# A decoder layer on one core: input laid out by features on the host, row factor spread by a product, first weight sums on VectorE, S5 three gaps later

## What is computed

```python
def rms_norm(x, g):
    xf = x.astype(F32)
    y = xf * lax.rsqrt(jnp.mean(xf * xf, axis=-1, keepdims=True) + EPS)
    return (y * g.astype(F32)).astype(x.dtype)
...
        xn = rms_norm(h, mix_norm_g[l])
        proj = jnp.einsum('bsd,de->bse', xn, w_in[l])
```

## Time and profile before

| | us |
|---|---|
| Median of the runs | 1942.64 |
| The profiled execution | 1942.32 |
| Its span, first to last instruction | 1939.6 |
| TensorE busy in the span | 1798.8 (93%) |
| VectorE busy | 781.7 (40%) |
| ScalarE busy | 241.8 (12%) |
| GpSimd busy | 178.6 (9%) |
| Mean granted TensorE clock | 0.971 of 2.4 GHz |

### The profile page before, as it was taken

The page is one execution under the profiler, slowest core; times in us unless marked ns, Lnnn a source line. Parts: engine busy times, 40 slices in busy tenths (PEclk is TensorE's granted clock), DMA queues, the critical chain, the costliest instruction groups (busy, mean ns, idle before and its releaser), DMA issues.

```text
span 1939.6 us, 30889 instructions
## 1 busy us (share of the span) xinstructions
PE 1798.8 (93%) x13021; PEld 1146.3 (59%) x13021; DVE 781.7 (40%) x1492; ACT 241.8 (12%) x552; POOL 178.6 (9%) x206
## 2 busy tenths in 40 slices
PE   6999999999999989999797679999999999999984
PEld 4888899889998879999642223323333333333321
DVE  7666684367457654333421112322222122221411
ACT  3012111200224421000110000000000000000021
POOL 1443342000000000000010000000000000000001
PEclk9999999999999999999898789999999999999988
DMA  6343333322121241422699999999999999999997
GB/s 221 98 140 88 99 89 89 100 66 66 47 90 55 71 171 66 162 79 66 259 377 427 426 425 425 426 426 424 421 425 424 422 425 427 425 426 421 416 411 317
DMA packets 67657, 506.13 MB, mean 261 GB/s; under 512 B 18903, under 2 KB 19051, under 8 KB 39927
## 3 DMA queue, kind: packets, MB, share of 16 engines
q1 hardware_dynamic: 49394, 476.21, 60.8%
q0 software_dynamic: 5728, 19.56, 2.9%
q10 hardware_dynamic: 12400, 8.36, 1.7%
HBM read 497.28 MB, written 14.04 MB: 264 GB/s over the span
## 4 chain that ended last, share of the span: by engine, by line
PE 71%; DMA 20%; DVE 4%; issue 2%; ACT 1%; SPq 1%; POOLq 0%; DVEq 0%; POOL 0%; ACTq 0%
PE psum L1008 20%; PE psum L1341 16%; PE psum L1011 16%; DMA arena<-in_moe_w_gate 14%; PE psum L1300 6%; PE psum L1378 4%; DMA arena<-in_moe_w_up 3%; DMA arena<-in_moe_w_down 2%; PE psum L1166 2%; DVE arena L1782 2%; PE psum L1067 1%; PE psum L1280 1%; DMA arena<-hs_rows,arena 1%; SPq L754 1%; PE psum L1197 1%
## 5 line engine op out<-in xcount | busy, mean ns | idle before, releaser
L1341 PE MATMUL psum<-arena 128*32 128x512 f32 x3584 | 416.5, 619 | 54.6 <-DMA arena<-in_moe_w_gate 26.2
L1008 PE MATMUL psum<-arena 128*128 128x128 f32 x3584 | 410.5, 276 | 0.0
L1008 PEld LDWEIGHTS psum<-arena 128*128 128x128 f32 x3584 | 405.2, 193 | 7.0 <-issue 6.4
L1782 DVE TENSOR_TENSOR arena<-psum,arena 128x512 f32<-128x512 f32 x305 | 203.3, 683 | 391.1 <-PE psum L1300 356.7
L1011 PE MATMUL psum<-arena 128*128 128x256 f32 x1456 | 322.4, 380 | 1.1 <-DVE arena L1782 1.1
L1341 PEld LDWEIGHTS psum<-arena 128*32 128x32 f32 x3584 | 119.0, 114 | 343.7 <-issue 335.4
L1011 PEld LDWEIGHTS psum<-arena 128*128 128x128 f32 x1456 | 273.6, 190 | 38.9 <-issue 2.1
L1782 DVE TENSOR_TENSOR arena<-arena,psum 128x256 f32<-128x256 f32 (+2 forms) x172 | 75.1, 437 | 415.5 <-PE psum L1008 215.6
L1378 PE MATMUL psum<-arena 128*32 128x512 f32 x1664 | 185.9, 605 | 18.8 <-DMA arena<-in_moe_w_down 18.7
L1782 DVE TENSOR_TENSOR arena<-arena 128x128 f32<-128x128 f32 (+17 forms) x452 | 181.0, 442 | 33.2 <-ACT arena L1517 25.3
L1300 PE MATMUL psum<-arena 128*128 128x512 f32 x416 | 191.9, 605 | 1.4 <-DVE arena L2425 1.4
(11 more groups left out here) (233 smaller groups left out, 1046.5 us busy)
## 6 DMA issues: line engine op xcount, KB each, us to landing
arena<-in_moe_w_gate SPq DMA_DIRECT2D x64, 2048.0 KB, 26.6
arena<-in_moe_w_up SPq DMA_DIRECT2D x64, 2048.0 KB, 24.6
arena<-in_moe_w_down SPq DMA_DIRECT2D x56, 2048.0 KB, 27.0
arena<-in_w_in SPq DMA_DIRECT2D x86, 512.0 KB, 4.6
arena<-in_w_out SPq DMA_DIRECT2D x32, 512.0 KB, 4.8
arena<-in_x SPq DMA_DIRECT2D x8, 1024.0 KB, 8.1
arena<-in_moe_w_down SPq DMA_DIRECT2D x8, 1024.0 KB, 18.5
arena<-in_moe_w_down SPq DMA_DIRECT2D x16, 512.0 KB, 12.1
```

What stands on the lines that cost most here:

```text
L1008: last = mm(B(bank, [(1, P)], off=t * P), F(a + t * P, P), F(w + i * P, P), start=start and t == 0, stop=(i == KH - 1), skip_group_check=True)
L1341: last = mm(B(bank, [(1, FE)], 32 * g, 32), F(xt + c * CAP + 32 * g, 32), F(SLOT[slot] + (c % 8) * FE, FE), start=(c == 0), stop=(c == KD ...
L1782: return v.tensor_tensor(o, a, b, op)
```

## The change

x is laid out by features on the host (`x_columns`, partition p holds features 16p to 16p+15, 512 tokens each) and loaded in six groups of 2, 2, 4, 4, 2 and 2 blocks, among the first two weight blocks. No transposes are left. VectorE multiplies each block by its gain alone (`gain`, 16 tensor_scalars of 128x512). The row factor comes later: ScalarE squares each group, GpSimd and VectorE fold the squares to 512 columns, TensorE sums them over the partitions by 28 products of one column (`square_sums`: 8 behind step k = 7, 20 ahead of k = 10), ScalarE takes the square root, VectorE the reciprocal times the identity (DIAG), and one product with ones spreads the factor over all partitions (`row_scales`, ahead of k = 12). u0 runs on the unscaled x and is scaled behind. VectorE scales A11, S1, A21, A12 and A22 by the spread factor and forms S2, S3, S4 from them. All four weight sums of the first pair are made on VectorE between these passes; disc_b and the two halves of the former lb part move behind products of the first two pairs. ScalarE's exponentials for lb and lambda move to ("fin", 0). The tables of S5, its blocks and the bias steps come three gaps later in the list: S5_START is 19. The last block then has y5 at gap 84, yt at 86, and ge, 89 by its distance, at 87. One semaphore of the router (order_ready) is joined with another (ranks_ready), with counts adjusted.

```diff
-S5_START = 16
+S5_START = 19
+XGROUPS = ((0, 2), (2, 4), (4, 8), (8, 12), (12, 14), (14, 16))
...
+        DIAG = XRAW
+        SQ = [CA, ST, S2, S4, UT, UT + 1024]
...
-        gaps[0] += [("T", 0, 0), ("T", 0, 1)]
-        gaps[1] += [("T", 0, 2), ("T", 0, 3)]
+        gaps[1].append(("ss",))
+        gaps[2].append(("bc",))
         for p in U_P + MID_P:
             gaps += products(p)
-        for k, st in ((5, [("ab",)]), (6, [("tb", 0)]), (7, [("tb", 1)]), (8, [("tb", 2)]), (9, [("cT", 0)]),
-                      (10, [("cT", 1)]), (11, [("cT", 2)]), (12, [("w1", 0, 0), ("w1", 0, 1), ("up", 0)]),
-                      (13, [("rb", 0), ("rb", 1), ("ca", 0, 0), ("ca", 0, 1)]), (14, [("br",)]), (16, [("bs",)])):
+        for k, st in ((8, [("ab",)]), (9, [("tb", 0)]), (10, [("tb", 1)]), (11, [("tb", 2)]), (12, [("cT", 0)]),
+                      (13, [("cT", 1)]), (14, [("cT", 2)]), (15, [("w1", 0, 0), ("w1", 0, 1), ("up", 0)]),
+                      (16, [("rb", 0), ("rb", 1), ("ca", 0, 0), ("ca", 0, 1)]), (17, [("br",)]), (19, [("bs",)])):
...
-            for t in range(TB):
-                sp.dma_start(F(XRAW + t * D, D), DV(d["x"], t * P * D, [(D, P), (1, D)])).then_inc(x_in[t], 16)
+
+            def x_group(g):
+                lo, hi = XGROUPS[g]
+                sp.dma_start(F(XRAW + lo * S, (hi - lo) * S),
+                             DV(d["x_columns"], lo * S, [(KD * S, P), (1, (hi - lo) * S)])).then_inc(x_in[g], 16)
...
+                for g in {0: (0,), 1: (1, 2), 2: (3, 4, 5)}.get(i, ()):
+                    x_group(g)
...
-            pool.wait_ge(x_in[TB - 1], 16)
+
+            def fold(g, n):
+                settle(g_tt(F(SQ[g], n), F(SQ[g], n), F(SQ[g] + n, n), ALU.add))
+
+            g_tt = g.tensor_tensor
+            pool.wait_ge(x_squared, 1)
+            fold(0, S)
+            pool.wait_ge(x_squared, 2)
+            fold(1, S)
+            pool.wait_ge(x_squared, 3)
+            fold(2, 2 * S)
+            fold(2, S)
+            pool.wait_ge(x_squared, 5)
+            fold(4, S)
...
+            def square_sums(tiles):
+
+                bank = use[("ss",)][0]
+                for i in tiles:
+                    if i == 3:
+                        pe.wait_ge(rst_parts, 1)
+                    elif i >= 5:
+                        pe.wait_ge(x_squared, 6)
+                    else:
+                        pe.wait_ge(pool_step, (1, 2, 4, None, 5)[i])
+                    x = SQ[min(i, 5)] + (i == 6) * S
+                    for t in range(TB):
+                        last = mm(B(bank, [(1, 1)], off=t), F(x + t * P, P), F(C["ones"], 1), start=(i == 0 and t == 0),
+                                  stop=(i == 6), skip_group_check=True)
+                    if i == 6:
+                        last.then_inc(full[bank], 1)
+
+            def row_scales():
+
+                bank = take_bank(pe, ("bc",))
+                pe.wait_ge(rst_parts, 2)
+                mm(B(bank, [(1, S)]), F(C["ones"], P), F(DIAG, S), start=True, stop=True).then_inc(full[bank], 1)
...
+                    if p == 0:
+                        once(xsum_ready, (1, 2, 3, 3, 5, 6, 7)[n])
...
+                    elif q == 3:
+                        row_scales()
                     w = see_block(pe, block_no[("u", 0, q // 2)])
                     for k in range(4 * q, 4 * q + 4):
+                        pe.wait_ge(x_gained, 2 + [lo <= k < hi for lo, hi in XGROUPS].index(True))
+                        if k == 10:
+                            square_sums(range(2, 7))
...
+            def square(g):
+                lo, hi = XGROUPS[g]
+                act.wait_ge(x_in[g], 16)
+                A(F(SQ[g], (hi - lo) * S), F(XRAW + lo * S, (hi - lo) * S), ACT.Square).then_inc(x_squared, 1)
+
+            act.wait_ge(x_gained, 1)
+            A(F(SM, 1), F(EPSC, 1), ACT.Exp)
+            square(0)
             act.wait_ge(disc_in, 48)
             A(V(DS + 2 * P, [(SN, 2), (1, SN)], 0, NQ), V(LDT, [(1, 2), (0, SN)], 0, NQ), ACT.Exp).then_inc(disc_act, 1)
+            square(1)
             act.wait_ge(disc_dve, 1)
             A(F(DS + 3 * P, P, 0, NQ), F(DS + 3 * P, P, 0, NQ), ACT.Exp).then_inc(disc_act, 1)
-
-            act.wait_ge(lb_dve, 1)
-            A(F(LBE, HH), F(LB, HH), ACT.Exp).then_inc(lb_act, 1)
-            act.wait_ge(lam_dve, 1)
-            A(F(LAME, 2), F(LAMD, 2), ACT.Exp).then_inc(lam_act, 1)
+            square(2)
             act.wait_ge(disc_dve, 2)
             A(F(DS + 7 * P, P, 0, NQ), F(DS + 6 * P, P, 0, NQ), ACT.Sin)
             A(F(DS + 8 * P, P, 0, NQ), F(DS + 6 * P, P, 0, NQ), ACT.Sin, scale=0.5).then_inc(disc_act, 1)
+            A(F(SM, 1), F(EPSC, 1), ACT.Sqrt)
+            for g in (3, 4, 5):
+                square(g)
+            bank = see_bank(act, ("ss",))
+            A(F(STD, TB), B(bank, [(1, TB)]), ACT.Sqrt, scale=1.0 / D, bias=F(EPSC, 1)).then_inc(free[bank], 1)
...
+                if s == ("fin", 0):
+                    act.wait_ge(lb_dve, 1)
+                    A(F(LBE, HH), F(LB, HH), ACT.Exp).then_inc(lam_act, 1)
+                    act.wait_ge(lam_dve, 1)
+                    A(F(LAME, 2), F(LAMD, 2), ACT.Exp).then_inc(lam_act, 1)
...
+                        act.wait_ge(xsum_ready, 4)
+                        act.dma_start(DV(u_d, 0, [(S, P), (1, S)]), F(UT, S)).then_inc(u_out[0], 16)
...
+            def gain(g):
+
+                lo, hi = XGROUPS[g]
+                dve.wait_ge(x_in[g], 16)
+                for k in range(lo, hi):
+                    last = ts(V((A11 if k < KH else A12) + (k % KH) * HB, [(A21 - A11, 2), (1, HB)]),
+                              V(XRAW + k * S, [(HB, 2), (1, HB)]), F(GMIX + k, 1), None, M)
+                last.then_inc(x_gained, 1)
...
+                if kind == "ss":
+                    see_copy(dve, s)
+                    settle(v.reciprocal(F(RST, TB), F(STD, TB)))
+                    tt(V(DIAG, [(P, TB), (1, P)]), V(IDENT, [(0, TB), (1, P)]), V(RST, [(1, TB), (0, P)]),
+                       M).then_inc(rst_parts, 1)
+                    settle(tt(F(S1, KH * HB), F(A21, KH * HB), F(A22, KH * HB), AD))
+                    weight_sum(dve, v, 0, 0)
+                elif kind == "bc":
+                    dve.wait_ge(u0_lo, 1)
+                    see_bank(dve, s)
+                    scaled(A11, 0).then_inc(xsum_ready, 1)
+                    settle(scaled(S1, 1))
+                    dve.wait_ge(xsum_ready, 1)
+                    tt(F(S2, KH * HB), F(S1, KH * HB), F(A11, KH * HB), SU).then_inc(xsum_ready, 1)
+                    weight_sum(dve, v, 0, 1)
+                    settle(scaled(A21, 1))
+                    tt(F(S3, KH * HB), F(A11, KH * HB), F(A21, KH * HB), SU).then_inc(xsum_ready, 1)
+                    weight_sum(dve, v, 0, 2)
...
+                    if s == ("pr", 0, 1):
+                        see_copy(dve, ("pj", "u", 0))
+                        u0 = V(UT, [(NC5, LC), (1, NC5)])
+                        tt(u0, u0, B(use[("bc",)][0], [(1, LC), (LC, NC5)]), M).then_inc(xsum_ready, 1)
+                        disc_b()
+                    elif s == ("pr", 0, 2):
+                        see_bank(dve, ("pj", "u", 0))
+                        scaled(A12, 0).then_inc(xsum_ready, 1)
+                        weight_sum(dve, v, 0, 3)
+                        scaled(A22, 1).then_inc(xsum_ready, 1)
+                        dve.wait_ge(xsum_ready, 6)
+                        bank = use[("bc",)][0]
+                        tt(F(S4, KH * HB), F(A12, KH * HB), F(S2, KH * HB), SU).then_inc(xsum_ready, 1)
+                        v.nop().then_inc(free[bank], 1)
+                    elif s == ("pr", 0, 3):
+                        bounds_a()
+                    elif s == ("pr", 1, 1):
+                        bounds_b()
...
+            dve.wait_ge(gains_in, 16)
+            gain(0)
+            dve.wait_ge(disc_in, 48)
+            settle(ts(R(0), R(0), -1e-4, None, ALU.min))
+            gain(1)
+            disc_a()
+            gain(2)
+            gain(3)
+            gain(4)
+            dve.wait_ge(x_squared, 4)
+            settle(tt(F(SQ[3], 2 * S), F(SQ[3], 2 * S), F(SQ[3] + 2 * S, 2 * S), AD))
+            tt(F(SQ[3], S), F(SQ[3], S), F(SQ[3] + S, S), AD).then_inc(rst_parts, 1)
+            gain(5)
...
+    arrays["x_columns"] = np.ascontiguousarray(whole["x"].T).reshape(P, KD * S)
```

More of the change, by code:

```diff
@@ L411, in build @@
         gaps.append([("ht", 7, 0), ("ht", 7, 1), ("lr",)])
-        steps = [("xT", t, q) for t in range(TB) for q in range(4)] + [s for gap in gaps for s in gap]
+        steps = [s for gap in gaps for s in gap]
         steps += [("rc",), ("rk",), ("ro",), ("rr",), ("id",)]
@@ L1093, in do @@
                 last = None
-                if kind == "xT":
-                    t, q = s[1:]
-                    once(ident_in, 16)
-                    once(x_scaled, t + 1)
-                    for c in range(4):
```

(48 more changed lines are left out.)

56 lines of the change are left out of this document (22 added, 34 removed).

## The result

| | Before | After |
|---|---|---|
| Median of the runs, us | 1943.18 (1941.6 to 1943.86, 6 runs) | 1951.18 (1949.04 to 1955.21, 6 runs) |
| Span of the profiled execution, us | 1939.6 | 1947.2 |
| TensorE busy, us | 1798.8 | 1806.3 |
| VectorE busy, us | 781.7 | 800.2 |
| Mean granted TensorE clock | 0.971 | 0.967 |

Ratio 1.0039, 95% interval 1.0028 to 1.0049: slower by 0.4%, about 8 us. The prediction said 1950.0, and slower with 0.73. The size is right; several terms in it are not, and two of them made up for each other.

A forecast was written before the change was run, and what follows sets the result against it. TensorE, busy throughout from 65.7 to 378.3 us, was taken as the bound. Front +1.1, GLU wait +5.2 and clock behind it +1.6 gave +7.9 on 1942.32: 1950 us, range 1942 to 1956 (the forecast's own 1946.7 to 1952.7).

The forecast's parts named there:

- The GLU's wait: Behind the last pair's product 6: the GELU runs behind fin's two sigmoids, so TensorE's GLU product waits, +5.2 us.
- The clock behind the stall: At the GLU: idle time lets TensorE's clock fall to half rate for some 3 us, +1.6 us.
- The first pair: Front, to the end of the first pair's seven products: -0.8 + 0.5 + 1.4 = +1.1 us against 65.34.
- GpSimd beside VectorE: Front: GpSimd adding squares slows VectorE's tensor_scalars, counting only at gain(2)'s end; 0 to 2 us, taken as 0.5.
- The load: Front: small S5 loads in by 9.3 us, gains through gain(2) done and steps 4 to 7 starting at 13.8.
- The clock: Front: waits and the squares' one-column products let TensorE's clock fall to half; 0 to 3.4 us, taken as 1.4.
- The middle: From first pair to GLU: S5 keeps its distances; the second pair costed at nothing, up to 2 us if VectorE is slower.
- (a): Rival: the front keeps its 7.2 us, the GLU's wait stays; 1941.9 us, no change; chance 0.10.
- (c): Rival: the front's gain reaches the end and S5's tail has slack; -7.2, 1935.1 us, faster; chance 0.09.
- (b): Rival: no wait at the GLU, front as worked out, +1.1; 1943.4 us, no change; chance 0.07.
- (d): Rival: slower still, clock and port at their ends, second pair stalled by 2; +13.4, 1955.7 us; chance 0.14.
- signs: Expected in the timeline: first 128x512 product near 6.5 us, TensorE idle for VectorE ahead of first-pair products 0, 1, 2, 4.

The follow-up runs named there:

- e1: The changed kernel with the last block's GELU one gap earlier (86), ahead of fin's two sigmoids on ScalarE; ratio to before 1.0014, 1946.92 us.
- e5: e1 with the gains of groups 1 and 2 and first squares ahead of waits for the small S5 loads, sines behind the square root; ratio to before 1.0019.
- e6: e1 with S1 and the first weight sum ahead of VectorE's wait for the square root; ratio to before 1.0013, 1946.09 us.
- e7: e1 with the squares' 28 products 128 columns wide instead of one; ratio to before 1.0014, 1946.79 us.
- e8: e1 with all three edits of e5, e6 and e7 together; ratio to before 0.9997, 1943.08 us.
- e10: e1 with the edits of e5 and e7, without that of e6; ratio to before 1.0011, 1946.12 us.
- e9: e8 with the second weight sum moved directly behind the diagonal on VectorE; ratio to before 0.9992, 1941.57 us.
- e2: The kernel before with only S5 and its tables moved three gaps later; ratio to before 1.0038, 1951.11 us.
- e3: The kernel before with S5 and its tables three gaps later and the last GELU in gap 86; ratio to before 1.0009, 1945.22 us.
- e4: The changed kernel with S5 and its tables where before has them (S5_START 16), so only the front is new; ratio to before 1.0074, 1958.13 us.
- e11: e9 with the shift of S5 and its tables cut to two gaps, last GELU again in gap 86; ratio to before 0.9990, 1942.04 us.

## Why the prediction was right, and where it was not

**The GLU's wait** was the decisive step, and it held: fin ahead of ge, with 3.72 us where it said 5.2. The mis-sized term is the first table load. The prediction took 1.28 for it from 378.94 in the earlier trace rows, where the GELU had come before. In the kernel after no GELU lies in between, the sigmoids' table is still in place, and they start at 380.67, 0.58 behind E. The load was counted twice: once where it had been, and once where it had gone to.

With the drain of the Trainium skill ("ScalarE: Activation LUTs", "What ACT_TABLE_LOAD costs") the prediction had a stall of 6.6 us. The trace doesn't agree: the load at 381.83 follows the sigmoids' end at 381.82, and the GELU follows the load by 0.02, so no drain is seen.

**The clock behind the stall**: 1.6 predicted, 1.7 measured.

**The first pair**: +1.1 predicted, +0.6 measured, and the nearness is luck. The sum took 0.5 for GpSimd beside VectorE and 1.4 for the clock. The first was too small, the second cost nothing, and together they came out right.

*The load.* Steps 4 to 7 start at 16.96 instead of 13.8. VectorE and ScalarE both wait for the last small load, 5.5 us, until 11.47; the prediction had it in at 9.3, from 5.3 us of flight in the earlier trace rows. Here it was 7.5 us in flight. Why isn't shown: the DMA engines moved 344 GB/s from 5 to 10 us, less than before. Then disc_a. The two rows of VectorE and GpSimd in after's timeline:

```profile
12.93 1.43 DVE L1835 TENSOR_SCALAR arena<-arena 20x128 f32<-20x128 f32 x2
12.88 1.40 POOL L790 TENSOR_TENSOR arena<-arena 128x512 f32<-128x512 f32 x1 [5.50 <-ACT arena L1577]
```

Such a tensor_scalar takes 0.21 alone (as a row at 47.87 shows); beside GpSimd's fold two take 1.43. The prediction looked for this only at the end of gain(2) and took 0.5. There it didn't come: eleven tensor_scalars, gain(2)'s among them, take 4.18 us from 15.01 on, beside GpSimd's folds. So the diagonal is ready 2.4 us late, near 29.7 instead of 27.3.

*The clock.* The half clock took 1.6 us in steps 10 and 11, near the 1.4 allowed, and the first chunk ends 4.1 later than the 32.0 worked out. But VectorE wasn't waiting for TensorE then, as its timeline shows:

```profile
29.04 2.90 DVE L1832 TENSOR_TENSOR arena<-arena 128x512 f32<-128x512 f32 x2
31.97 1.23 DVE L592 TENSOR_TENSOR arena<-arena 128x1024 f32<-128x1024 f32 x1
33.12 4.48 DVE L1832 TENSOR_TENSOR arena<-arena,psum 128x2048 f32<-128x2048 f32 x2
```

These are the diagonal and S1, the first weight sum, and the scaling of A11 and S1, with no idle time between them. The spreading product ends at 32.87, ahead of 33.12, so its lateness cost VectorE nothing, and product 0, at 36.14, found A11 ready. This is the step that failed: the prediction added the clock's loss on TensorE to the end of the first pair, while from the scaling of A11 on VectorE's chain sets that end, and here its start didn't wait for TensorE's spreading product. The eight kernels with the new front and the shift by three gaps show it (us):

| Kernel | Scaling of A11 starts | First pair ends | Between |
|---|---|---|---|
| after | 33.12 | 65.94 | 32.8 |
| e1 | 31.98 | 64.81 | 32.8 |
| e5 | 37.91 | 70.74 | 32.8 |
| e6 | 34.02 | 66.85 | 32.8 |
| e7 | 35.15 | 67.97 | 32.8 |
| e8 | 30.02 | 63.38 | 33.4 |
| e10 | 32.55 | 65.91 | 33.4 |
| e9, second weight sum ahead of it | 30.41 | 62.11 | 31.7 |

With the clock low or full ahead of product 0, the distance is the same. The rest of the span, behind the first pair, is 1876.0 to 1877.3 us in e1 and e5 to e10, so what sets their profiled executions apart is this chain, above all when it starts. Its start is VectorE's own work in after, e1, e7 and e10, and the spreading product in e6 and e8, where VectorE waits 4.06 and 1.38 us for it. The prediction had 30.8 for its start and 33.7 for its length: the start came 2.3 late, the chain was 0.9 shorter, and -0.8 + 1.4 is the +0.6. The products wait 4.3 us in all, not 7.4, mostly because TensorE itself came late. VectorE's prices held: 2.24 for a scaled 2048 columns (2.3 predicted), 2.29 for a pair, 1.22 for a weight sum.

The Trainium skill ("SBUF — State Buffer", section "SBUF: two separate sides") calls VectorE's and GpSimd's common port an exclusive lock. The pair of rows at 12.9 us agrees: VectorE's 1.43 us end within 0.1 of GpSimd's 1.40.

**The middle**: costed at nothing, measured +1.3. The shift puts the tables of S5, VectorE's work, into other gaps, and a weight sum is late by 0.7 us between 120 and 180 us. e2 and e3 show it on the old front too. Another 0.36 is the cT transpose that the prediction took out of the figure to beat and didn't count again behind the first pair. The last 0.2 stays open.

**The rivals.** (a) and (c) fell: the first pair ends at 65.9. (b), no wait at the GLU, is what e1 makes of it: 1.0014 there, against the 1943.4 (1.0004) worked out. Between them are 1.9 us; the middle, which the sum has at nothing, is 1.3 of these, and the interval takes in the rest. (d) stayed in the range; no 2 us in the second pair. The forecast's own upper bound was added up wrong: by its terms it is 1953.7, not 1952.7. Of the signs, TensorE's waits stand ahead of products 1, 2 and 4 but not of product 0, and the first 128x512 product came at 8.31 instead of 6.5, behind the first weight block, hidden behind the wait for gain(2).

What stays open: when the clock falls. After and e1, e4, e5 and e6 have the same one-column products. The first window of theirs below 1.00 is from 28 us in after and e1, from 24 in e4 and e6, and from 20 in e5. Behind the same wait of 1.97 us ahead of product 2 the clock fell in e8 and e10 and stayed at 1.00 in after, e1, e5, e6 and e7. If it varies so between executions of one kernel as well, it would be part of why the runs of after lie 6 us apart; that was not measured.

## What to carry to other kernels

Where steps stand at fixed distances on a list with an end, look at what a shift does to the last of them: here a step that fell on the last place was appended behind a wait, and that alone cost more than half of the loss. Where two engines hand work to each other, edits that each shorten one engine's way can each show nothing and together some 3 us: follow both chains to the point where they meet, and make the experiment with both. Before a loss on one engine goes into a sum, look whether the other is late at the meeting point anyway. And a wait that is gone from a trace is a gain only if the work ahead of it didn't become slower. And an engine's idle time ahead of a handed-over factor is the place for work that doesn't need it.

## What the runs showed of the hardware

- TensorE's granted clock fell to 0.50 (1.2 of 2.4 GHz) behind one-column products while TensorE was busy without a gap (after: busy 8.00 of 8.00 us from 20 to 28, then 0.66 and 0.50 to 32). All five kernels with these products show it between 20 and 32 us. With 128 columns in the same 20 products it stayed at 1.00 from 20 to 36 us in all five that have them (e7, e8, e9, e10, e11). The width is all but free: 4.63 us for 40 instructions in e7 and 4.52 in after.
- Behind a wait of 1.97 us, with another one product earlier (1.32 in e8, 2.03 in e10), the clock was below 1.00 for some 6 us, down to 0.50. It stayed at 1.00 behind the like waits in after, e1, e5, e6 and e7 (e6: 1.31 and 1.97; e7: 2.03 and 1.97).
- VectorE's tensor_scalar slows down beside GpSimd even at 20 partitions by 128: 1.43 us for two that take 0.21 each. It isn't always so: eleven, most of them of 128x512, took 4.18 us beside GpSimd's folds, 0.38 each, and three folds of 128x1024 took 10.01 there where two took 3.81 in e8.
- Behind a wait of 3.7 us, 128x512 products ran at 0.50 and then 0.74 for 4 us (384 to 388 in after).
